# A two-layer hybrid decoder trunk on one core: norms moved behind their projections, attention threaded between projections, output weights cut in halves

## The reference

```python
h = x
# even layer
proj = rmsnorm(h, g0) @ w_in_even                 # 1024 -> 2560: q, k, v, ub, vb (512 each)
oa = rmsnorm(p1 @ v - lam * p2 @ v, subln) * 0.8  # 4 heads; p1, p2: causal softmax of q1 k1, q2 k2; partial rotary
vb = layernorm(gelu(vb)); ob = gelu(ub) * (tril(sgu_w) @ vb + sgu_b)   # in chunks of 128 positions
h = h + concat(oa, ob) @ w_out_even
y = rmsnorm(h, g1); h = h + (silu(y @ wg) * (y @ wu)) @ wd             # hidden 2816
# odd layer
proj = rmsnorm(h, g2) @ w_in_odd                  # xc (512), cq (384), ckv (256), kpe (32)
oc = (window means of xc - xc) @ pool_w * pool_scale                   # windows 2, 4, 8, 16
q = rmsnorm(cq) @ w_uq; kv = rmsnorm(ckv) @ w_ukv                      # 8 heads, rotary on 32 channels
od = causal attention(q, [k, kpe], v)
h = h + concat(oc, od) @ w_out_odd
y = rmsnorm(h, g3); the 2 best of 8 experts (hidden 3584) by y @ router; h = h + sum gate_e * swiglu_e(y)
return rmsnorm(h, final_norm)
```

## Time and profile before

| | us |
|---|---|
| median of three runs | 1546.31 |
| the profiled execution's own time | 1543.57 |
| its span, first to last instruction | 1541.8 |
| first large product starts | 16.22 |
| first FFN product starts | 157.33 |
| last FFN product ends, by the chain | 349.13 |
| first expert's products start, by the chain | 511.94 |

### The profile page before, as it was taken

One profiled execution on the slowest core, in us unless ns is written; L12 is line 12 of the kernel. 1 busy time (PEld: TensorE's weight loads), 2 busy tenths in 40 slices (PEclk: granted clock), 3 DMA queues, 4 the chain that ended last, 5 costly groups with the idle time before them and its releaser, 6 DMA issues.

```text
span 1541.8 us, 20148 instructions
## 1 busy us (share of the span) xinstructions
PE 1437.3 (93%) x7038; PEld 1197.6 (78%) x7039; DVE 1171.2 (76%) x1203; ACT 1009.9 (65%) x1155; POOL 14.0 (1%) x25
## 2 busy tenths in 40 slices
PE   6977999997787999999999999999999999999995
PEld 5755999986576788788888878888888887887884
DVE  5645454454545899899899899989989989988994
ACT  5433444444533777777787787777778777778773
POOL 2000000000000000000000000000000000000000
PEclk9978899998977899999999999999999999999998
DMA  9513454453416699899899899989989999998940
GB/s 338 189 55 109 158 183 174 155 185 119 176 55 233 245 374 364 295 370 370 324 343 368 326 341 364 373 296 370 370 294 375 368 326 334 373 366 296 373 164 27
DMA packets 176932, 420.91 MB, mean 273 GB/s; under 512 B 3664, under 2 KB 7760, under 8 KB 176896
## 3 DMA queue, kind: packets, MB, share of 16 engines
q1 hardware_dynamic: 175344, 415.40, 73.9%
q0 software_dynamic: 1552, 5.02, 1.1%
HBM read 419.36 MB, written 1.05 MB: 273 GB/s over the span
## 4 chain that ended last, share of the span: by engine, by line
PE 90%; DVE 5%; ACT 2%; issue 2%; DVEq 1%; DMA 0%; ACTq 0%
PE ps L1209 24%; PE ps L1211 24%; PE ps L1210 24%; PE ps L1368 3%; PE ps L1369 3%; PE ps L1370 3%; PE ps L1460 2%; PE ps L1491 2%; PE ps L1278 1%; PE ps L1222 1%; DVE w_lo L1112 1%; DVE h L1184 1%; ACT xn L463 1%; PE ps L1240 1%; PE ps L1529 0%
## 5 line engine op out<-in xcount | busy, mean ns | idle before, releaser
L1112 DVE TENSOR_TENSOR w_lo<-ring_a,w_hi 128x1024 fp32r<-128x1024 f32 x384 | 458.1, 1223 | 38.8 <-ACT w_hi L661 29.8
L661 ACT ACTIVATE w_hi<-ring_a 128x1024 fp32r<-128x1024 f32 x384 | 399.7, 1059 | 75.5 <-PE ps L1211 74.6
L1112 DVE TENSOR_TENSOR w_lo<-ring_b,w_hi 128x1024 fp32r<-128x1024 f32 x288 | 346.5, 1224 | 33.3 <-ACT w_hi L661 26.4
L1209 PE MATMUL ps<-w_hi,xg_hi 128*128 128x512 f32 x896 | 359.2, 401 | 9.9 <-DVE w_lo L1112 9.0
L1211 PE MATMUL ps<-w_hi,xg_lo 128*128 128x512 f32 x896 | 353.9, 395 | 0.0
L1210 PE MATMUL ps<-w_lo,xg_hi 128*128 128x512 f32 x896 | 353.9, 395 | 0.0
L661 ACT ACTIVATE w_hi<-ring_b 128x1024 fp32r<-128x1024 f32 x288 | 301.4, 1058 | 58.5 <-PE ps L1211 58.5
L749 DVE TENSOR_TENSOR w_lo<-ring_a,w_hi 128x1024 fp32r<-128x1024 f32 (+2 forms) x119 | 140.5, 1193 | 134.2 <-ACT w_hi L453 134.0
L453 ACT ACTIVATE w_hi<-ring_a 128x1024 fp32r<-128x1024 f32 (+2 forms) x119 | 121.6, 1032 | 137.0 <-PE ps L1370 69.7
L1209 PEld LDWEIGHTS ps<-w_hi,xg_hi 128*128 128x128 f32 x896 | 168.8, 188 | 51.2 <-DVE w_lo L1112 12.5
L1211 PEld LDWEIGHTS ps<-w_hi,xg_lo 128*128 128x128 f32 x896 | 169.0, 189 | 39.8
(11 more groups left out here) (261 smaller groups left out, 1469.2 us busy)
## 6 DMA issues: line engine op xcount, KB each, us to landing
ring_a<-in_moe_wg SPq DMA_DIRECT2D x40, 2048.0 KB, 7.9
ring_a<-in_moe_wu SPq DMA_DIRECT2D x32, 2048.0 KB, 8.0
ring_b<-in_moe_wd SPq DMA_DIRECT2D x32, 2048.0 KB, 7.8
ring_b<-in_moe_wu SPq DMA_DIRECT2D x24, 2048.0 KB, 8.5
ring_a<-in_moe_wd SPq DMA_DIRECT2D x24, 2048.0 KB, 7.7
ring_b<-in_moe_wg SPq DMA_DIRECT2D x16, 2048.0 KB, 7.8
ring_a<-in_ffn_wg SPq DMA_DIRECT2D x5, 2048.0 KB, 8.9
ring_a<-in_ffn_wu SPq DMA_DIRECT2D x5, 2048.0 KB, 7.6
```

The source lines that it names most:

```text
L661: nc.scalar.activation(w_hi[:, (Q1 + q) % NQ, 0:1024], slot(j % RING2)[:, 1024 * k:1024 * k + 1024], ACT.Copy).then_inc(hi_done, 1)
L1112: v.tensor_tensor(w_lo[:, (Q1 + q) % NQ, 0:1024], slot(j % RING2)[:, 1024 * k:1024 * k + 1024], w_hi[:, (Q1 + q) % NQ, 0:1024].bitcast(F32 ...
L1209: pe.matmul(out_, a_hi, w_hi[:, q, c0:c1], start=first, stop=False)
```

## The change

The dense part (all ahead of the experts) is written anew; the experts' loop is the same.

1. The norms ahead of the projections are no longer applied to h. TensorE transposes h itself; the gain is a scale by partition (`gcol`, the gains transposed once at the start) when the tile leaves PSUM, and the reciprocal root is a scale by row when the projection leaves PSUM (`RSTD`). In the FFN it is a row of 256 numbers (`rrow`, made by a product of ones and a diagonal) by which VectorE multiplies the gate before the silu, one instruction more in each chunk; the up part's factor is put in when down's sum goes into h. The same for cq and ckv.
2. The even layer's order is q, k, vb, ub, v. The transposes of q and k, the scores, the probabilities and the gating stand between the quanta of later projections. The two maps are joined before the values (`combine`), so there are half as many transposes and values.
3. The layernorm of vb is applied by GpSimd, six instructions.
4. The output weights are cut in two halves by rows. Those of the part that is ready first (gating, pooling) are used ahead of the attention's result; the attention's half follows in two column blocks, and the transposes of h for the next norm stand inside the second.
5. The FFN has its order of before; only its opening and its end change: the last down unit is cut in two column halves, so that the first half of h can be added and transposed while the second is multiplied.
6. The odd layer is ordered cq, ckv, `w_uq`, `w_ukv`, pool, with the attention between the quanta of pool and the first half of the output.
7. The router multiplies transposed h by `rwg` (router times gain) and the factor is put in at the softmax; the lo part of the experts' input is written after the choice of slots (line 1273).

The pieces below are, in this order, the units, ScalarE's small loads, GpSimd's layernorm, ScalarE's scaled hi part, VectorE's joining of the maps, TensorE's order in block ub, and VectorE's FFN.

```diff
-    for b in (4, 3, 0, 1, 2):
-        add("in_even", columns(w_in_e, 512 * b, 512 * b + 512), (KC, 512), 1024)
+    for name, b in (("q", 0), ("k", 1), ("vb", 4), ("ub", 3), ("v", 2)):
+        add(name, columns(w_in_e, 512 * b, 512 * b + 512), (KC, 512), 1024)
+    add_out("oe", A["w_out_even"][0])
...
+            for name in GCOLS:
+                act.dma_start(grow[a:a + k, :], A[name][0].rearrange("(c p) -> c p", p=P)).then_inc(grow_in, 16)
...
+            pool.wait_ge(ln_ready, 1)
+            for t in range(T):
+                pool.tensor_scalar(vg, vg, st("ROOT", t, 1), st("LNBIAS", t, 1), ALU.mult, ALU.add).then_inc(ln_step, 1)
+                pool.tensor_tensor(vg, vg, gain[:, 0:512], ALU.mult).then_inc(ln_step, 1)
+                pool.tensor_tensor(vg, vg, gain[:, 512:1024], ALU.add).then_inc(ln_applied, 1)
...
+            def head(name, f, dst, chunks=2, base=0, g=None, each=None):
+                act.wait_ge(*filled(k))
+                    for c in range(chunks):
+                        ins = copy(dst[:, c0 + c, :], src[:, c, :], ACT.Copy, scale=gcol[:, at:at + 1])
...
+            def combine(ee, qt):
+                dve.wait_ge(exped, qt + 1)
+                for m in range(4):
+                    ins = v.scalar_tensor_tensor(out=ee[:, m, 0:w], in0=ee[:, 4 + m, 0:w], scalar=st(inv, 4 + m, 1),
+                                                 in1=ee[:, m, 0:w], op0=ALU.mult, op1=ALU.add)
...
+            for kq in range(4):
+                pe.wait_ge(lo_done, q + 1)
+                projection(q, kq, 512, (2, 3)).then_inc(q_used, 1)
+                if kq == 0:
+                    scores_first(qT, kT, A_QK, 4)
+                elif kq < 3:
+                    pe.wait_ge(sc_read, kq)
+                    scores_second(qT, kT, A_QK, 4, kq - 1)
+                else:
+                    pe.wait_ge(ln_applied, 2)
...
             for f, w in enumerate(widths):
-                dve.wait_ge(fsilu, f + 1)
-                v.tensor_tensor(x, x, ps[:, 0:c, 256:512], ALU.mult).then_inc(fmul, 1)
+                v.tensor_tensor(x, ps[:, a:a + c, 0:256], row.to_broadcast([P, c, S]), ALU.mult).then_inc(fgate, 1)
+                dve.wait_ge(fsilu, f + 1)
+                v.tensor_tensor(x, x, ps[:, a:a + c, 256:512], ALU.mult).then_inc(fmul, 1)
```

More of the change, by code:

```diff
@@ new lines, in _ @@
+            exponentials(0, e, 0, range(4))
+            hi_upto(b + 6)
+            exponentials(0, e, 0, range(4, 8)).then_inc(exped, 1)
+            hi_upto(end("ub") + 4)
+            act.wait_ge(q_used, end("ub"))
+            for t in range(T):
+                ins = copy(proj[:, t, 1536:2048], ps[:, 2 + t, :], ACT.Gelu_apprx_tanh, scale=st("RSTD", t, 1))
+            ins.then_inc(evacuated, 1)
+            b = first("v")
+            hi_upto(b + 5)
+            exponentials(0, e, 1, range(4))
@@ new lines, in _ @@
+            ins.then_inc(evacuated, 1)
+            b = first("oe_mix")
+            hi_upto(b + 5)
+            k = fills["p1_a"] + 1
+            evac(k, eT[:, 1, 0:4, :], ps[:, 6 + k % 2, :].rearrange("p (m s) -> p m s", m=4))
+            hi_upto(b + 7)
+            root(3, 8)
+            hi_upto(b + 8)
+            for f in range(2):
+                head("oa", f, xt_hi, base=4, each=st("SUBC"))
+            hi_upto(end("oe_att", 0) + 3)
+            act.wait_ge(h_done, 1)
+            half_sums(0)
@@ new lines, in wide, with residual @@
+            def wide(name, at, n, u):
+                return st(name, at, n).rearrange("p (m u) -> p m u", u=1).to_broadcast([P, n, u])
+            def residual(half, done, banks, scale=False):
+                dve.wait_ge(q_used, done)
+                for t in range(T):
+                    hb = h[:, t, 512 * half:512 * half + 512]
+                    src = ps[:, banks[t] + half * (banks[2]), :]
+                    if scale:
+                        ins = v.scalar_tensor_tensor(out=hb, in0=src, scalar=st("RSTD", t, 1), in1=hb, op0=ALU.mult,
+                                                     op1=ALU.add)
+                    else:
+                        ins = v.tensor_tensor(hb, hb, src, ALU.add)
+                ins.then_inc(down_added if scale else h_done, 1)
@@ L955, in _ @@
-            rests("ffn", (xt_hi, xt_lo, KC))
+                v.tensor_tensor(oa[:, t], oa[:, t], wide("ROOT", 4 * t, 4, P), ALU.mult).then_inc(oa_done, 1)
+            lo_upto(b + 8)
+            for f in range(2):
+                rest("oa", f, (xt_hi, xt_lo), base=4, each=st("SUBC"))
+            lo_upto(end("oe_att", 0) + 3)
+            residual(0, end("oe_att", 0), (2, 0, 1))
+            lo_upto(end("oe_att", 1) + 3)
+            for f in range(2):
+                rest("ffn", f, (xt_hi, xt_lo), g="norm_ffn_even")
@@ new lines, in _ @@
+            pe.wait_ge(od_done, 2)
+            for f in range(2):
+                turn("od", f, lambda c, t: proj2[:, t, P * c:P * (c + 1)])
+            for half in range(2):
+                for kq in range(2):
+                    if half == 0:
+                        pe.wait_ge(*emptied(fills["od"] + kq))
+                    attention_rows(first("oo_att", half) + kq, kq, half, odd_out)
+                    if half == 1 and kq == 0:
+                        pe.wait_ge(h_done, 3)
+                        for f in range(2):
+                            turn("router", f, h_chunk)
```

1456 lines of the change are left out of this document (858 added, 598 removed).

## The result

The changed kernel takes 1472.87 us (median of four runs, 1471.63 to 1474.26), the kernel before 1547.66 in the same set: a ratio of 0.9516, 95% interval 0.9498 to 0.9534, so 4.8% less. The forecast was 1489.3, 3.7% less. The profiled execution took 1473.97 with a span of 1472.2, and against the profiled one of before that is 69.6 less where 57.0 were forecast.

The account below looks back on a forecast made before the run. TensorE was taken as the bound, with time to gain only where it stands still or runs at half clock; 31.6 - 1.4 + 28.7 - 1.9 = 57.0 us less gives 1486.6 profiled, 1489.3 as median; range 1472 to 1513.

Parts of the forecast that it names:

- the cover is complete: Rival: GpSimd and the pooling and softmax copies are on time, waits mostly go, about 17 us more gained: 1472; chance 0.15.
- Start, 14.0: Up to TensorE's first product: it starts at 14.0 us in place of 16.22, bounds 11.2 and 17.
- Even layer, 111.7: First product to the FFN: 101.1 us of TensorE work plus late items and half clock make 111.7, before 141.1.
- GpSimd: Even layer: gating products wait for six GpSimd instructions, 10.1 us at 1.68 each against 6.8 of cover: 3.4 waited.
- The head norm: Even layer's output product: the attention's half waits for the norm of its last tile, 3.0 us.
- The half clock: Even layer: one of the waits is long enough to drop TensorE's clock, 1.7 us lost.
- FFN, +1.4: FFN: opening -1.6 for clock, +1.7 for transposes and row products, first chunk's wait +1.3; sum +1.4 us.
- FFN's end to the router's products, 112.8: Odd layer: work 96.5, late items 12.9, two half-clock spells 3.4; sum 112.8 us, 28.7 less.
- Router, +1.9: Between choice and gather: both lo parts, 2.36 us, are now waited for, ranks lose 0.5: +1.9.
- Experts, 0: Experts' stage: left alone by the change, 1029.9 us before, nothing gained or given back.
- ScalarE's queue as the breaking thread: Rival: ScalarE's jobs between some 45 quanta's splits make `w_hi` late by 0.6 us on the mean: 1516; chance 0.20.
- The ring falling behind: Rival: quanta split only after the threaded step ahead, 121 us exposed for 53 quanta outside the FFN: 1610; chance 0.05.

Follow-up runs that it names:

- the second trace of the same kernel: The changed kernel itself run once more, unaltered, beside other versions on one chip: 1474.68 us (0.9522).
- The halved chunk: Against the changed kernel, the first FFN chunk's multiplications and silu run in two halves of 512 columns, silu's table loaded ahead: 1470.06 us (0.9500).

## The prediction against this

It was right in direction, mechanism and range (1472 to 1513), and too cautious by 16 us, so that it lies inside its range by 0.9 only. The measured time is what the rival *the cover is complete* gave, 1472, and its reason, waits and half clock that mostly go, was the right one for half of the miss (5.4 us in the even layer, 3.9 in the odd one). That its number was met is luck: the rest is 3.7 us of work put too high in the two layers, 2.9 of the experts and some 4 between the traces and the medians, none of which it argued, less 3.3 by which the start and the FFN were dearer.

- *Start, 14.0.* Measured 15.14. The gains landed at 7.8, within the bound; the table load stood on the path as feared, and all four pairs of transposes stand ahead of the first product, of which the sum had one.
- *Even layer, 111.7.* Measured 105.05. The work was put at 101.1 and is 99.9. What was mis-sized is the late items and the half clock, 10.6 together; measured, 5.2. GpSimd: 8.0 long and not 10.1, with 7.9 of cover and not 6.8, so 0.15 for 3.4. ScalarE's gating hi part: 1.1 for 2.5. The head norm: 1.5 and 1.1 for 3.0. The half clock: 0 for 1.7 in this trace. That is chance: in the second trace of the same kernel the head norm's waits had it behind them and it cost 1.2, so the item was sound.
- *What the page of the Trainium skill gave.* By the Trainium skill's GPSIMD Engine Reference, section 3.1, the prediction made the six about 6.5 and the item nothing; its two figures add up to 6.0 (four of 1.12 and two of 0.77, an estimate), and the other 0.5 was given no source. The trace has 0.77 once for the one-input form, as the Trainium skill states, but 1.74 the second time, and 1.30 for the two-input one where a quarter of its figure is 1.12. Measured 7.7 in instructions. The result by the Trainium skill (nothing waited) was nearer than mine: 0.15 was.
- *FFN, +1.4.* Measured +3.6. The wait behind the first chunk was put at 3.7 and is 4.8; the loss behind it was taken to be that of before, about 1.7, and is 2.5 (26 products at 0.213 for 0.117). The halved chunk shows both.
- *FFN's end to the router's products, 112.8.* Measured 106.4, and 104.6 in the second trace. Idle 9.0 for 12.9, work 2.5 less; the half clock is the 3.4 forecast in the first trace (two spells, in the opening and at the router's products) and half as much in the second, which has only the later one.
- *Router, +1.9.* Measured +1.8.
- *Experts, 0.* Measured -2.9. Nothing in the argument could give this: the step took it that untouched code keeps its time. It keeps its instructions, not its buffers' addresses.
- *The rivals.* ScalarE's queue as the breaking thread fell: 64 us more of its work cost 24 to 26, and TensorE waited for no split. The ring falling behind fell with it; its 53 quanta are 55.

The medians moved 5 us more than the profiled executions, since that of before was 4.1 below its median and that of the changed kernel 1.1 above.

## What to carry over

Where one engine is the bound and its gaps are latencies of norms and softmaxes, price the threading by walking the queues, and then test the walk's late items for a common bias: here nearly all inside the two attentions were too dear, and those of the start and of the first FFN chunk too cheap. Look for the item that is just in time rather than for the busy engine: GpSimd, busy 17 us of 1472, has no slack at all, ScalarE, busy 1016, had some forty beside the dense blocks. Read the clock in more than one trace: a spell at half clock that is missing from one can stand in the next of the same instructions. Before a stage that a change does not touch is booked at nothing, see whether the change moves its buffers.

## What was not expected of the hardware

- With 1024 bytes of unused space ahead of the experts' buffers each product that streams `w_lo` is 2 ns shorter, 0.4 us of 126.9 for an expert, 2.9 us in all.
- A wait of 2.4 us brought half clock behind it before, 4.8 us brought 5.7 us of it in one trace and less in the next, 2.2 us at the same place none. Waits of 2.1 to 2.4 us elsewhere, and the two of 1.5 and 1.1 us around eight transposes at the head norm, had it in one trace and not in the next of the same instructions. Those that were seen behind these waits cover 2.7 to 5.7 us and cost 1.2 to 2.6, and the changed kernel's runs lie up to 4 us apart; that these are the spells is likely and not shown.
- From 15.1 to 19.1 the products of the changed kernel start 0.43 us apart, where 0.23 is their pace later, while the granted clock reads 1.00: the column does not show this spell, which costs about 1.8. The kernel before has three such products there.
- The one-input instruction of GpSimd took 0.77 and then 1.74 in one queue, on the same shape; beside the second a split on VectorE took 2.03 in place of 1.22. That the two slow each other is likely and not shown.
